# The first stage of a two-block transformer kernel: halves of 512 columns, a linear weight by weight, x scaled ahead of turning

## Chip, core and metric

One NeuronCore of a Trainium2 chip runs the whole program in one launch. The metric is the device time of one execution in microseconds (us). All arithmetic is float32; the large products are made of three products of float32 parts each (a high part in the engine's rounded format `fp32r`, and a low part that is the rest), so each weight and each activation has to be split into a high and a low part before TensorE may use it.

## The reference, cut to what matters

Two transformer blocks on `x` of 512 tokens by 1024 features, one batch. Only the beginning concerns this change:

```python
cond = silu(c)                                 # c: 1024 numbers
mod = cond @ w_ada[i] + b_ada[i]               # w_ada[i]: 1024 x 6144
sh1, sc1, gt1, sh2, sc2, gt2 = split(mod, 6)   # six vectors of 1024
h = rmsnorm(x, g_mix[i]) * (1 + sc1) + sh1     # modulate
cq = rmsnorm(h @ w_dq, g_q)                    # 1024 -> 384
q = cq @ w_uq                                  # 384 -> 8 heads x 192
ckv_kr = h @ w_dkv                             # 1024 -> 256 + 64
kv = rmsnorm(ckv_kr[..., :256], g_kv) @ w_ukv  # 256 -> 8 heads x 256
```

The angles of the rotary embedding (sine and cosine of position times frequency) are computed too. Behind this come attention, its output product, two feed-forward parts, a windowed attention, and the second block; the change leaves them alone.

## The kernel before, in words

The kernel holds x turned, with features on the partitions (`X`, 8 chunks of 128 features by 512 tokens). Each engine has its own program, written out by hand in order; an engine waits on named counts (`wait_ge`), in that order, so whatever stands behind a waiting instruction on its engine waits too. `Slots` hands out PSUM banks and small tiles in turn.

Weights are loaded by SyncE in the order of `PLAN` into three raw buffers (`SLOT`, `OLD`: a buffer is loaded again once its old content is used). ScalarE makes each weight's high part (`act_split`), VectorE the low part (`dve_split`), TensorE uses both.

The first stage, `*_begin` (lines 996 to 1087): x (2 MB) is loaded as one piece, turned by TensorE and copied out by ScalarE; ScalarE squares it, GpSimd sums the squares, TensorE sums them over partitions, and the reciprocal roots are spread over the partitions by a diagonal and a product (`R`). Of the two vectors that the first norm needs, the scale (vector 1) is made on VectorE in eight steps of 128x1024 (`dve_ada`), each a multiply and add with one column of silu(c), then summed over partitions by TensorE; the shift (vector 0) is made on TensorE as row products (`pe_row`). Each is loaded in four pieces of 1 MB. `dve_normed` then forms x times gain times `R` chunk by chunk, ScalarE adds the shift and makes the high part, VectorE the low part, for the first 256 tokens and then for the others.

The first linear, `dq`, is 1024 to 384: two weight units of four chunks. `pe_linear` goes by halves of the tokens on the outside and by weights inside: 4 x 36 products of 128x256. `dkv` follows in the same way, then `uq` (blocks of two heads; two of them here), then `ukv` in two blocks. TensorE's order is in `pe_mla_in` (line 1268), VectorE's in `dve_mla_in` (1353), GpSimd's in `pool_mla_in` (1405).

Three more vectors of `w_ada` (2, 4, 3) are made beside this: `BESIDE` has their 24 pieces of 128x1024. GpSimd's queue loads a piece (`pool_beside`, 719), VectorE takes it in one step (`dve_beside`, 730). The first eight pieces are vector (0, 2). TensorE sums it in `pe_columns(e, 0, 2)` (699), which waits for the eighth, and which stands in its order between the second `uq` block and `ukv`.

GpSimd computes the angles in `pool_begin` (1094), some 25 instructions of 128x512.

Of the kernel before, what the change touches and what calls it, by code (L numbers as in the profile page):

```python
# [146 lines left out]
def bass_two_blocks(nc, A, out):  # L147
    ctx = ExitStack()
    with ctx:
# [63 lines left out]
        XIN = sb([128, 4, D], F32, AR)  # L213
        V1 = sb([115, 128], F32, AR + 16 * KB)
# [150 lines left out]
        ada(0, 1)  # L365
        ada(0, 0, kind="p")
# [92 lines left out]
        FIRST, LAST = 8, WT[WX["mo"][3]]["p"]  # L459
        SLOT, OLD, held = [], [], {}  # L460
        for p in range(len(PLAN)):
            SLOT.append((p - FIRST - 1) % 2 if FIRST < p <= LAST else p % NRAW if p <= FIRST else (p - LAST) % NRAW)
            OLD.append(held.get(SLOT[p]))
            held[SLOT[p]] = p
        BESIDE = [(0, v, k) for v in (2, 4, 3) for k in range(8)]
# [55 lines left out]
        c_in, const_in, x_in, vec_in = count("c_in"), count("const_in"), count("x_in"), count("vec_in")  # L521
# [423 lines left out]
        def dve_add_x(e, T, j, hf, b, key, scale, before, mods=()):  # L945
# [9 lines left out]
                  mods=[(mod, (0, 1)), (mod, (0, 0))], h_free=lambda hf: (), h32=None)  # L955

        def act_vectors(e):
            A_ = {"c": A["c"].rearrange("b (j p) -> (b j) p", p=128),
# [13 lines left out]
            for name, (r, k) in rows.items():  # L972
                if name == "bq":
# [4 lines left out]
            e.dma_start(V2[:, :], A["b_ada"].rearrange("l (j p) -> (l j) p", p=128)).then_inc(vec_in, by=16)  # L978
            e.dma_start(VEC[:, 115:116], A["k_invf"]).then_inc(vec_in, by=16)
            e.dma_start(POS[:, :], A["positions"].to_broadcast([128, S])).then_inc(vec_in, "all", by=16)  # L980

        def pe_row(e, p, l, v, u):
            raw = raw_of(p, 2, D)
            e.wait_ge(landed[SLOT[p]], p)
            e.wait_ge(cond, "silu")
            for kk in range(2):
                k = 2 * u + kk
                for hf in range(2):
                    if k == 0:
                        banks.take(("row", hf), (copied, ("row", hf)), keep=True)  # L990
                        e.wait_for(banks.free(("row", hf)))
                    t = e.matmul(PS[0:1, banks["row", hf], :], SILUC[:, k:k + 1], raw[:, kk, 512 * hf:512 * hf + 512],
                                 start=k == 0, stop=k == 7)
            t.then_inc(acc, ("row", p))

        def pe_begin(e):
# [16 lines left out]
            pe_row(e, 4, 0, 0, 0)  # L1013
            pe_row(e, 5, 0, 0, 1)
            e.wait_ge(misc, "ones")
            pe_sums(e, "n0", 0, lasthf=F, add=ssq_pool)
            pe_sums(e, "n0", 1, lasthf=F, add=ssq_pool)
            pe_mod(e, 0, 1)
            pe_row(e, 6, 0, 0, 2)
            pe_row(e, 7, 0, 0, 3)  # L1020
            b = banks.take("row", (mod, (0, 0)))
            e.wait_for(banks.free("row"))
            for hf in range(2):
                e.wait_ge(copied, ("row", hf))
                for j in range(4):
                    t = e.matmul(PS[:, b, 4 * hf + j:4 * hf + j + 1],
                                 TMP[ta["row", hf]][0:1, 128 * j:128 * j + 128], ones[0:1, 0:1], start=True, stop=True)
                t.then_inc(acc, ("row", "t", hf))
                banks.open(("row", hf))
            for hf in range(2):  # L1030
                pe_R(e, n0, hf)
                banks.open(("R", "n0", hf))

        def act_begin(e):
            act_vectors(e)
            e.wait_ge(acc, "c")
            e.activation(SC[:, :], PS[:, banks["c"], 0:8], ACT.Exp, scale=-1.0).then_inc(misc_act, "exp")
            for j in range(8):
                e.wait_ge(acc, ("x", j))
                e.activation(X[:, j, :], PS[:, banks["x", j], :], ACT.Copy).then_inc(x_init, j)  # L1040
                e.wait_ge(x_init, j)
                act_square(e, "n0", j, F, X[:, j, :], add=ssq_pool)
            act_mod(e, 0, 1)
            act_root(e, "n0", 0, D)
            act_root(e, "n0", 1, D)
            act_split(e, 0)
            e.wait_ge(acc, ("row", 7))
            for hf in range(2):
                s = ta.take(("row", hf), (acc, ("row", "t", hf)))
                e.wait_for(ta.free(("row", hf)))  # L1050
                e.activation(TMP[s][0:1, :], PS[0:1, banks["row", hf], :], ACT.Copy).then_inc(copied, ("row", hf))
            act_normed(e, n0, 0, ALL)
            act_split(e, 1)
            act_normed(e, n0, 1, ALL)
            ta.hand([(h_lo, ("n0", 7, 1))], 4)
            ta.only(0, 1, 2, 4)

        def dve_begin(e):
# [4 lines left out]
            e.memset(ZERO, 0.0).then_inc(misc, "zero")  # L1063
            e.wait_ge(misc_act, "exp")
# [5 lines left out]
            for _ in range(4):  # L1070
                dve_item(e)
# [4 lines left out]
            e.wait_ge(misc, "columns")  # L1076
            dve_mod_lo(e, 0, 1)
            dve_diag(e, "n0", 0)
            dve_diag(e, "n0", 1)
            dve_mod(e, 0, 1)  # L1080
            dst = MOD[:, 0, 0:8]
            dve_split(e, 0)
            e.wait_ge(acc, ("row", "t", 1))
            e.tensor_tensor(dst, PS[:, banks["row"], 0:8], dst, ALU.add).then_inc(mod, (0, 0))
            dve_normed(e, n0, 0, ALL)
            dve_split(e, 1)
            dve_normed(e, n0, 1, ALL)
# [6 lines left out]
        def pool_begin(e):  # L1094
            for j in range(1, 7):
                add_square(e, "n0", j, F, add=ssq_pool)
# [8 lines left out]
            e.wait_ge(vec_in, "all")  # L1105
# [3 lines left out]
            for dst, quarter in ((SIN, 0.0), (COS, 0.25)):  # L1109
                ts(PA[:, :], PB[:, :], 1.0 / TWO_PI, quarter, ALU.mult, ALU.add)  # L1110
# [200 lines left out]
        def act_mla_in(e):  # L1311
            sums0 = lambda N: [(acc, ("sum", N, 0)), (acc, ("sum", N, 1))]
# [2347 lines left out]
```

## Time and profile before

| | |
|---|---|
| time, median of 3 runs | 2256.89 us (2255.12 to 2258.03) |
| the profiled execution | 2252.95 us |
| its span in the profile | 2250.9 us |
| mean granted TensorE clock | 0.992 |
| TensorE busy | 2181.1 us, 97% of the span |
| VectorE, ScalarE, GpSimd busy | 63%, 43%, 8% |
| moved by DMA | 245.70 MB, 109 GB/s in the mean |

The profile is of one execution. The page gives for each engine its busy time and for each group of instructions count and mean duration; the chain that ended last is followed back from the last instruction and says, for each moment, what the end was waiting for. A line of the kernel such as L66 is that of a helper, so all products have L66, all activations L72. "PE" is TensorE, "DVE" VectorE, "ACT" ScalarE, "POOL" GpSimd, "SP" SyncE.

### The profile page before, as it was taken

To read this page: it belongs to the slowest core of one execution; us is meant where nothing else is said; L and a number is where in the kernel's file an instruction comes from. 1 tells how busy PE (TensorE), PEld (TensorE's weight loads), DVE (VectorE), ACT (ScalarE), POOL (GpSimd) and SP (SyncE) were. 2 spreads that over 40 slices of the span, in tenths; PEclk is the share of its full clock that TensorE was granted. 3 is DMA by queue.
4 is the path that set the end of the run, shared out by engine and by line. 5 is a ranking of instruction groups with operands and counts; after the bars stand their busy time and mean duration, and the time that the engine had idled before them with its cause. 6 is when DMAs were issued, how large, how long until landed. Compare 5 with 4: busy or idle time off the path is not lost.

```text
span 2250.9 us, 31890 instructions
## 1 busy us (share of the span) xinstructions
PE 2181.1 (97%) x13239; PEld 1927.5 (86%) x13239; DVE 1418.2 (63%) x2129; ACT 965.0 (43%) x1460; POOL 184.9 (8%) x159
## 2 busy tenths in 40 slices
PE   6999999999999999999999999999999999999999
PEld 3877988888898898898898999997778889899998
DVE  5777565656577667565556667754665545666674
ACT  3556442213256645453443434434444334443443
POOL 7310000000032100000020000002012001000001
PEclk8999999999999999999999999999999999999999
DMA  6542245555521122332421332323112332233231
GB/s 237 162 145 90 89 169 187 187 189 185 187 83 57 39 66 85 113 99 90 132 75 62 113 105 96 109 89 111 52 47 80 122 105 64 66 122 106 88 108 56
DMA packets 128325, 245.70 MB, mean 109 GB/s; under 512 B 4843, under 2 KB 36934, under 8 KB 128054
## 3 DMA queue, kind: packets, MB, share of 16 engines
q1 hardware_dynamic: 123424, 228.02, 30.3%
q0 software_dynamic: 4096, 15.28, 2.1%
q8 instruction: 105, 1.72, 0.3%
q10 hardware_dynamic: 662, 0.37, 0.1%
q14 instruction: 38, 0.31, 0.0%
HBM read 241.56 MB, written 2.10 MB: 108 GB/s over the span
## 4 chain that ended last, share of the span: by engine, by line
PE 83%; DVE 9%; ACT 3%; DMA 2%; issue 2%; POOL 0%; SPq 0%; DVEq 0%; ACTq 0%
PE PS L66 82%; DVE t L75 5%; ACT t L72 3%; DVE t L83 2%; DVE t L86 1%; DMA t<-in_ffn_w_dram 1%; PE PS L69 1%; DMA t<-in_w_ada_dram 1%; DVE t L79 1%; DMA t<-in_w_ff_dram 0%; DVE t L92 0%; DVE t L80 0%; POOL t L75 0%; SPq L101 0%; DVE PS L75 0%
## 5 line engine op out<-in xcount | busy, mean ns | idle before, releaser
L66 PE MATMUL PS<-t,t 128*128 128x256 f32 (+4 forms) x12872 | 2134.1, 328 | 38.8 <-DMA t<-in_w_ada_dram 8.7
L66 PEld LDWEIGHTS PS<-t,t 128*128 128x128 f32 (+2 forms) x12872 | 1884.0, 188 | 285.0 <-issue 50.4
L72 ACT ACTIVATE t<-t 128x1024 fp32r<-128x1024 f32 (+7 forms) x738 | 654.3, 903 | 935.2 <-DVE t L75 462.1
L75 DVE TENSOR_TENSOR t<-t,t 128x1024 fp32r<-128x1024 f32 (+9 forms) x693 | 778.2, 1139 | 377.6 <-ACT t L72 330.6
L72 ACT ACTIVATE t<-PS 128x512 f32<-128x512 f32 (+4 forms) x327 | 174.9, 549 | 216.8 <-PE PS L66 166.1
L75 POOL TENSOR_TENSOR t<-t,t 128x512 f32<-128x512 f32 (+2 forms) x71 | 86.2, 1215 | 1091.2 <-ACT t L72 932.9
L75 DVE TENSOR_TENSOR t<-t,PS 128x512 f32<-128x512 f32 (+2 forms) x134 | 83.1, 625 | 145.5 <-PE PS L66 139.2
L72 ACT ACTIVATE t<-t,t 128x256 fp32r<-128x256 f32 (+5 forms) x220 | 115.8, 535 | 95.7 <-DVE t L83 44.8
L83 DVE SCALAR_TENSOR_TENSOR t<-t,t,t 128x1024 f32<-128x1024 f32 (+2 forms) x157 | 144.4, 926 | 16.7 <-DMA t<-in_w_ada_dram 11.0
L83 DVE SCALAR_TENSOR_TENSOR t<-PS,t,t 128x512 f32<-128x512 f32 (+3 forms) x128 | 82.1, 648 | 87.8 <-PE PS L66 82.2
L75 DVE TENSOR_TENSOR t<-t 128x512 f32<-128x512 f32 (+4 forms) x104 | 74.2, 714 | 16.2 <-ACT t L72 15.8
L83 DVE SCALAR_TENSOR_TENSOR t<-PS,t 128x512 f32<-128x512 f32 (+1 forms) x84 | 49.3, 610 | 53.1 <-PE PS L66 53.1
L69 PE MATMUL PS<-t,t 128*128 128x128 f32 (+1 forms) x367 | 56.9, 297 | 26.3 <-DVE t L79 8.3
L69 PEld LDWEIGHTS PS<-t,t 128*128 128x128 f32 (+1 forms) x367 | 45.5, 153 | 33.4 <-issue 11.3
L83 DVE SCALAR_TENSOR_TENSOR t<-t,t,PS 128x256 f32<-128x256 f32 (+1 forms) x117 | 54.4, 488 | 17.1 <-PE PS L66 14.1
L79 DVE TENSOR_SCALAR t<-t,t 128x128 f32<-128x128 f32 (+5 forms) x163 | 59.3, 394 | 4.5 <-DMA t<-in_w_ada_dram 2.5
L79 POOL TENSOR_SCALAR t<-t 128x512 f32<-128x512 f32 x28 | 46.5, 1662 | 74.3 <-DVE t L86 50.0
L79 POOL TENSOR_SCALAR t<-t,t 128x512 f32<-128x512 f32 x13 | 23.9, 1853 | 327.8 <-DVE t L83 312.8
L86 DVE CUSTOM_DVE_ANT_0 t<-PS,t 128x128 f32<-128x128 f32 (+1 forms) x112 | 38.4, 352 | 13.8 <-PE PS L66 13.7
L75 DVE TENSOR_TENSOR t<-PS,t 128x512 fp32r<-128x512 f32 (+2 forms) x40 | 24.9, 633 | 31.8 <-ACT t L72 24.7
L101 POOL DMA_DIRECT2D t<-in_k_dist_dram x1 | 0.5, 543 | 421.5 <-PE PS L66 421.5
L72 ACT ACTIVATE t<-PS,t 128x2 f32<-128x2 f32 (+3 forms) x48 | 21.5, 453 | 26.2 <-PE PS L66 22.0
(30 smaller groups left out, 166.9 us busy)
## 6 DMA issues: line engine op xcount, KB each, us to landing
t<-in_w_ff_dram SPq DMA_DIRECT2D x64, 1024.0 KB, 5.2
t<-in_ffn_w_dram SPq DMA_DIRECT2D x60, 1024.0 KB, 5.1
t<-in_w_ada_dram SPq DMA_DIRECT2D x36, 1024.0 KB, 6.4
t<-in_w_ada_dram POOLq DMA_DIRECT2D x24, 512.0 KB, 4.5
t<-in_w_in_dram SPq DMA_DIRECT2D x12, 1024.0 KB, 5.1
t<-in_swa_w_qkv_dram SPq DMA_DIRECT2D x6, 1024.0 KB, 5.7
t<-in_ffn_w_dram SPq DMA_DIRECT2D x8, 768.0 KB, 4.4
t<-in_w_in_dram SPq DMA_DIRECT2D x24, 256.0 KB, 3.6
```

The lines of the kernel that those rows point to most:

```text
L66: return Instr(self.real and self.real.matmul(o, lhs, rhs, start=start, stop=stop, **more))
L69: return Instr(self.real and self.real.transpose(o, src, ident))
L72: return Instr(self.real and self.real.activation(o, src, func, **more))
L75: return Instr(self.real and self.real.tensor_tensor(o, a, b, op))
L79: return Instr(self.real and self.real.tensor_scalar(o, a, s1, s2, op0))
L83: return Instr(self.real and self.real.scalar_tensor_tensor(o, a, s, b, op0, op1))
L86: return Instr(self.real and self.real.tensor_tensor_reduce(**more))
L101: return Instr(self.real and self.real.dma_start(o, src))
```

## The change

What it does, part by part:

- SyncE loads x in four pieces and the two vectors in four halves of 512 columns, (1,0), then (0,0) and (1,1), then (0,1) (vector, half), four pieces of 512 KB each, between the first weights, into tiles of their own, with no wait. The vectors leave `PLAN`.
- VectorE makes both vectors, `dve_first`: 32 steps of 128x512. The row products go.
- VectorE squares x as loaded and sums over features in one instruction for 128 tokens (`tensor_tensor_reduce`). ScalarE multiplies x, tokens on partitions, with its reciprocal root (`XSC`), TensorE turns this too, ScalarE applies the gain as it copies out (`act_gain`), for the upper four chunks in a second pass (`act_gain_again`). `R` and its diagonals go, for this norm.
- The first linear goes weight by weight (`pe_dq`): unit 0 for both token halves, then unit 1 for both. Products of the last vector halves stand in between. Four products whose result nothing uses (`warm`) stand ahead.
- GpSimd's angles start with the positions, which are loaded first on ScalarE's queue; two pieces of `BESIDE` are loaded between sine and cosine.
- The two single `dve_beside` steps in VectorE's `dq` and `dkv` parts go, and two come behind its second `uq` block.

```diff
-        ada(0, 1)
-        ada(0, 0, kind="p")
...
-        FIRST, LAST = 8, WT[WX["mo"][3]]["p"]
+        FIRST, LAST = 0, WT[WX["mo"][3]]["p"]
...
+        FIRST_PARTS = {0: ((1, 0),), 1: ((0, 0), (1, 1)), 2: ((0, 1),)}
...
+        def dve_first(e, v, ch, ks):
+            buf, tile = (ACC if v else ACC0)[:, 512 * ch:512 * ch + 512], FIRST_TILES[v, ch]
+            for k in ks:
...
+                    e.tensor_scalar(buf, tile[:, k, :], c, None, ALU.mult).then_inc(ada_acc, (0, v, ch, k))
+                else:
+                    e.wait_ge(ada_acc, (0, v, ch, k - 1))
+                    e.scalar_tensor_tensor(buf, tile[:, k, :], c, buf, ALU.mult, ALU.add).then_inc(ada_acc, (0, v, ch, k))
...
         def act_begin(e):
             act_vectors(e)
...
+            e.wait_ge(x_sq, 3)
+            e.activation(RS[:, 0:4], RS[:, 0:4], ACT.Sqrt, bias=EPSC, scale=1.0 / D).then_inc(root, "n0")
+            e.wait_ge(recip, "n0")
+            for t4 in range(4):
+                e.activation(XSC[:, t4, :], XIN[:, t4, :], ACT.Copy, scale=RS[:, t4:t4 + 1]).then_inc(x_gain, t4)
             for j in range(8):
                 e.wait_ge(acc, ("x", j))
                 e.activation(X[:, j, :], PS[:, banks["x", j], :], ACT.Copy).then_inc(x_init, j)
...
+            act_gain(e, LOWER)
             act_split(e, 0)
+            act_gain(e, (4, 5))
+            act_first_hi(e, 0, LOWER)
+            act_gain(e, (6, 7))
+            act_first_hi(e, 1, LOWER)
+            act_gain_again(e, UPPER)
             act_split(e, 1)
+            act_first_hi(e, 0, UPPER)
+            act_first_hi(e, 1, UPPER)
...
+            dve_first(e, 0, 0, range(2))
+            dve_first_columns(e, 1, 0)
+            dve_first(e, 0, 0, range(2, 6))
+            dve_at["vec"] = (0, 0)
             dve_split(e, 0)
+            dve_first(e, 0, 0, range(6, 8))
+            dve_first_columns(e, 0, 0)
+            dve_lowered(e, 0, LOWER)
+            dve_first(e, 1, 1, range(4))
+            dve_lowered(e, 1, LOWER)
+            dve_first(e, 1, 1, range(4, 8))
+            dve_first(e, 0, 1, range(2))
+            dve_first_columns(e, 1, 1)
+            dve_first(e, 0, 1, range(2, 4))
             dve_split(e, 1)
+            dve_first(e, 0, 1, range(4, 8))
+            dve_first_columns(e, 0, 1)
+            dve_lowered(e, 0, UPPER)
+            dve_lowered(e, 1, UPPER)
...
             for hf in range(2):
                 if hf:
                     dve_diag(e, "cq", 0, place=DIAG[0][0])
-                    dve_beside(e)
...
                     dve_diag(e, "cq", 1, place=DIAG[0][1])
-                    dve_beside(e)
...
             dve_uq(e, 1, WX["ukv"][0], after0=ck, after1=kr)
+            dve_beside(e, 2)
             dve_columns(e, 0, 2)
...
+            for t4 in range(4):
+                e.dma_start(XIN[:, t4, :], A["x"][0, 128 * t4:128 * t4 + 128, :]).then_inc(x_in[t4], "x", by=16)
```

## Rows read from the trace of the kernel before

**Rows 1.** The page: the span, and the chain that ended last by engine.
```profile
span 2250.9 us, 31890 instructions
...
PE 83%; DVE 9%; ACT 3%; DMA 2%; issue 2%; POOL 0%; SPq 0%; DVEq 0%; ACTq 0%
```

**Rows 2.** The chain of waits from 0 to 140: start us, us, what.
```profile
49.27 7.84 PE PS L66 x36
...
58.21 42.38 PE PS L66 x319
...
110.10 2.06 issue
...
114.15 22.11 PE PS L66 x90
```

**Rows 3.** Timeline of ScalarE from 71 us: start, us, instruction [idle before, releaser].
```profile
72.31 0.38 ACT L72 ACTIVATE t<-PS 128x256 f32<-128x256 f32 x1 [0.61 <-PE PS L66]
```

**Rows 4.** Windows: each engine's busy time, then PEclk, DMA share, GB/s.
```profile
5.00:10.00 5.00, 0.35 (x2) 0.35 (x3) 0.54 (x3) 1.46 (x2) 0.00 (x0) 1.00 1.03 407
10.00:15.00 5.00, 5.00 (x26) 5.00 (x25) 2.04 (x2) 4.07 (x8) 1.64 (x1) 1.00 1.04 363
```

**Rows 5.** Timeline of TensorE from 9 us: x is turned.
```profile
9.65 6.17 PE L69 MATMUL PS<-t,t 128*128 128x128 f32 x32 [5.60 <-DMA t<-in_x_dram]
```

**Rows 6.** Groups by shape on ScalarE and VectorE: count, busy us, mean ns, idle before.
```profile
L72 ACT ACTIVATE t<-t,t 128x1024 f32<-128x1024 f32 x4 | 4.6, 1149 | 2.2 <-DVE t L79 2.2
L72 ACT ACTIVATE t<-PS 128x512 f32<-128x512 f32 x220 | 128.9, 591 | 179.6 <-PE PS L66 133.9 <-PE PS L69 25.9 <-issue 8.6
L72 ACT ACTIVATE t<-PS,t 128x512 f32<-128x512 f32 x6 | 3.9, 686 | 8.6 <-PE PS L66 5.1 <-PE PS L69 3.2 <-DVE t L95 0.2
L72 ACT ACTIVATE t<-t,t 128x512 f32<-128x512 f32 x20 | 14.4, 720 | 17.4 <-DVE t L79 14.3 <-DVE t L95 2.9
L72 ACT ACTIVATE t<-t 128x1536 fp32r<-128x1536 f32 x18 | 26.5, 1475 | 13.3 <-PE PS L66 9.3 <-DMA t<-in_mla_w_dq_dram 4.0
L72 ACT ACT_TABLE_LOAD x15 | 19.2, 1283 | 8.1 <-issue 7.9
...
L75 DVE TENSOR_TENSOR t<-t,t 128x1024 fp32r<-128x1024 f32 x168 | 204.8, 1222 | 44.2 <-ACT t L72 38.7
L75 DVE TENSOR_TENSOR t<-t,t 128x1536 fp32r<-128x1536 f32 x18 | 31.7, 1768 | 31.1 <-ACT t L72 30.9
L79 DVE TENSOR_SCALAR t<-t,t 128x1024 f32<-128x1024 f32 x15 | 11.2, 750 | 2.7 <-DMA t<-in_w_ada_dram 2.5
L86 DVE CUSTOM_DVE_ANT_0 t<-PS,t,t 128x512 f32<-128x512 f32 x8 | 6.0, 751 | 0.3
L83 DVE SCALAR_TENSOR_TENSOR t<-t,t,t 128x512 f32<-128x512 f32 x8 | 5.4, 744 | 0.0
```

**Rows 7.** Timelines of GpSimd and of VectorE at three places.
```profile
17.13 2.12 POOL L75 TENSOR_TENSOR t<-t,t 128x512 f32<-128x512 f32 x1
...
50.47 0.48 DVE L83 SCALAR_TENSOR_TENSOR t<-t,t,t 128x256 fp32r<-128x256 f32 x1
...
77.12 1.28 DVE L83 SCALAR_TENSOR_TENSOR t<-t,t,t 128x1024 f32<-128x1024 f32 x1
```

**Rows 8.** Line L83 on VectorE from 16 to 29: ns min/median/max, first and last start.
```profile
L83 DVE SCALAR_TENSOR_TENSOR t<-t,t,t x6: 1511/2099/2167, 16.2 to 27.0; 128x1024 f32<-128x1024 f32 x6
```

**Rows 9.** Windows of 1 us, columns as in rows 4.
```profile
49.00:50.00 1.00, 0.73 (x3) 0.71 (x3) 0.96 (x3) 0.33 (x1) 1.00 (x1) 0.50 0.00 0
...
114.00:115.00 1.00, 0.89 (x3) 0.76 (x3) 1.00 (x3) 0.28 (x1) 0.00 (x0) 0.50 0.72 240
...
117.00:118.00 1.00, 1.00 (x6) 0.83 (x5) 1.00 (x3) 1.00 (x3) 0.00 (x0) 0.94 0.00 0
```

**Rows 10.** Timeline of VectorE from 98 to 118.
```profile
109.96 2.27 DVE L75 TENSOR_TENSOR t<-t,t 128x2048 fp32r<-128x2048 f32 x1
...
115.39 1.41 DVE L75 TENSOR_TENSOR t<-t,t 64x512 fp32r<-64x512 f32 x2
```

More of the change, by code:

```diff
@@ L213, in bass_two_blocks @@
         XIN = sb([128, 4, D], F32, AR)
+        JUNK = [sb([128, D], F32, o_lo + 4 * i * KB) for i in range(2)]
+        XSC = sb([128, 4, D], F32, o_hi + 8 * KB)
+        HN0 = sb([128, 8, S], F32, o_h + 16 * KB)
+        ACC0 = sb([128, D], F32, o_tmp)
         V1 = sb([115, 128], F32, AR + 16 * KB)
@@ L977, in act_vectors @@
                     e.dma_start(V1[r:r + k, :], A_[name]).then_inc(vec_in, by=16)
[L978 to L994, printed above, removed]
+            e.dma_start(V2[:, :], A["b_ada"].rearrange("l (j p) -> (l j) p", p=128)).then_inc(vec_in, "all", by=16)
@@ new lines, in pe_first_columns @@
+        def pe_first_columns(e, v, ch):
+            b = banks.take(("mod", 0, v, ch), (mod, (0, v, "sum", ch)))
+            e.wait_for(banks.free(("mod", 0, v, ch)))
+            e.wait_ge(ada_acc, (0, v, ch, 7))
+            e.wait_ge(misc, "ones")
+            for j in range(4):
+                t = e.matmul(PS[:, b, j:j + 1], (ACC if v else ACC0)[:, 512 * ch + 128 * j:512 * ch + 128 * j + 128],
+                             ones[:, 0:1], start=True, stop=True)
+            t.then_inc(acc, ("mod", 0, v, ch))
@@ L1023, in pe_begin @@
[L1023 to L1032, printed above, removed]
+            pe_x_scaled(e, LOWER)
@@ new lines, in pe_begin, with pe_x_scaled @@
+            pe_first_columns(e, 1, 0)
+            pe_x_scaled(e, UPPER)
+            b = banks.take("warm", (acc, "warm"))
+            e.wait_for(banks.free("warm"))
+            e.wait_ge(landed_first[0, 0][1], (0, 0))
+            for _ in range(4):
+                t = e.matmul(PS[:, b, :], ones, X[:, 0, :], start=True, stop=True)
+            t.then_inc(acc, "warm")
+            pe_first_columns(e, 0, 0)
+        def pe_x_scaled(e, chunks):
+            for j in chunks:
+                b = banks.take(("xs", j), (x_turned, j))
+                e.wait_for(banks.free(("xs", j)))
+                for t4 in range(4):
+                    e.wait_ge(x_gain, t4)
+                    t = e.transpose(PS[:, b, t4 * 128:(t4 + 1) * 128], XSC[:, t4, j * 128:(j + 1) * 128], ident)
+                t.then_inc(acc, ("xs", j))
@@ L1034, in act_begin, with act_first_hi @@
+        def act_first_hi(e, hf, chunks):
+            for j in chunks:
+                cs = COLS[hf]
+                if j in UPPER:
+                    e.wait_ge(x_gain, ("again", j))
+                e.wait_ge(x_turned, j)
+                e.wait_ge(mod, (0, 0, "sum", j // 4))
+                e.activation(HHI[:, j, cs], HN0[:, j, cs], ACT.Identity, bias=MOD[:, 0, j:j + 1]).then_inc(
+                    h_hi, ("n0", j, hf))
         def act_begin(e):
             act_vectors(e)
-            e.wait_ge(acc, "c")
@@ L1069, in dve_begin @@
             e.tensor_tensor(SILUC[:, :], PS[:, banks["c"], 0:8], SC[:, :], ALU.mult).then_inc(cond, "silu")
-            for _ in range(4):
-                dve_item(e)
+            dve_x_squares(e, range(2, 4))
+            dve_first(e, 1, 0, range(2))
+            e.wait_ge(root, "n0")
+            e.reciprocal(RS[:, 0:4], RS[:, 0:4]).then_inc(recip, "n0")
+            dve_first(e, 1, 0, range(2, 8))
             e.wait_ge(acc, "columns")
```

169 lines of the change are left out of this document (113 added, 56 removed).

## The prediction

> **What bounds the kernel now.** I read the page first: TensorE holds 83% of the chain that ended last [rows 1], so a change pays only where TensorE waits. Next the chain of waits in order of time, from 0 to 140 us. The reader is to see that TensorE does not work steadily before 49.27 (until then the chain is loads of `w_ada`, the row products and their copies), that the first unit of `dq` takes 7.84 us for 36 products, that from 58.21 it runs without a break to 100.6, and that a second hole comes at 110.10, 2.06 us before the `ukv` products [rows 2]. Then ScalarE's timeline: the last third of `dq` is copied out at 72.31, 0.61 us after waiting for TensorE, so `dq` ends at T = 72.3 [rows 3]. From T to the end of the first `ukv` block the rest of the program keeps its order, with one exception that the diff makes (below). So the change has two terms: A, how far T moves; B, what the exception costs.
>
> **Loads.** The queue now has x (2.1 MB), two vectors in four halves (2.1 MB each) and the weights between them, and no wait ahead of any. The queue moves 407 and 363 GB/s when it has enough to do [rows 4]; at 0.39 MB per us behind x (landed 9.65, when its turning starts [rows 5]) the halves have landed at about 15, 22.4, 27.8 and 35.2, `dq` at 17 and 29.8. Each of the steps below comes later than its data after 15 us, so loads stop setting the pace. That the smaller pieces cost nothing is bounded by the two rows: at the slower rate throughout the last half lands at 36.8, still unneeded.
>
> **A, step by step** (durations [rows 6] unless said).
> 1. Squares of x, four reductions of 1024 columns on VectorE. The trace has none of that width: bounds 1.22 (a subtraction of 1024) and 1.50 (twice the 512 one, 0.75); I take 1.37, between them. The last one ends at 11.4.
> 2. Table load 1.28, root and reciprocal 0.43: 13.2.
> 3. ScalarE scales x in four of 1.15: 17.8, copies the turned x out in eight of 0.59: 22.5. These eight stand in front of the gain, since the order is fixed. A bank for the first small products comes free only near their end; gain there at 23.2 (0.7, my estimate from four weight loads and two small adds).
> 4. Four gains from PSUM at 0.69: 26.0; the first weights' high part 1.48: 27.5; VectorE's low part 1.77: 29.3; two steps of the second half vector, 0.74 each: 30.8; its products and addition 1.0: 31.8; shift and low part of one chunk 1.0: TensorE starts `dq` at 32.8, where it was 49.27.
> 5. But the unit after it waits for the upper halves, and these go on VectorE after the lower ones. From 32.3: four low parts 2.0, eight steps of half (1,1) and two of (0,1) with four more low parts between them: 2.64 + 1.95 + 2.98 + 1.16 = 8.7, product and gain 0.5: 43.5. (A half vector costs one 0.38, half of the 0.75 of 1024, rounded up to 0.42 for its start, and seven 0.74: 5.6. Four cost 22.4. Before, VectorE had one vector, 0.75 + 7 x 1.28 = 9.7 us, and TensorE the other, so this adds 12.7 us of work to VectorE.)
> 6. ScalarE's gains again 4 x 0.72 = 2.9, weights 1.48, low part 1.77, four steps 3.0, product and addition 1.0, shift and low part 1.0: 11.2, and 54.7.
> 7. VectorE beside GpSimd. A step of 1024 takes 1.28 alone, and a median of 2.10 while GpSimd adds in SBUF (its addition 2.12) [rows 7, 8]: each such addition costs VectorE 0.8. Beside a GpSimd instruction with one tensor in, the 256-column steps keep their 0.48 [rows 7]. The table of angles used to start behind GpSimd's additions of squares; now it starts near 6 and its cosine half (three additions, 11 instructions, about 18 us) runs from about 31 to 49, just over steps 5 and 6. Bounds: 0 (all in VectorE's idle time) and 3 x 0.8 plus as much again for the one-input ones, 4.8. I take 2.2: 56.9.
> 8. TensorE has been idle for over 9 us then. Its granted clock is 0.50 when it starts at 49 (the 1.2 GHz level); after the hole at 110 it is 0.50 at 114 and up at 117 [rows 9]. The unit's first half took 7.84 before (bound above); 36 at the full pace of 0.12 would be 4.3 (below; 108 products from 58.21 to T). No product here is held by VectorE after the fourth, so about 3 us of low clock: 6.4. The second half at full pace 4.6. T' = 67.9.
> A = 67.9 - 72.3 = -4.4. Bounds from the open prices: -4.4 - 2.2 - 2.1 - 1 = about -10, and -4.4 + 2.6 + 1.4 = about 0. Removed row products, diagonals and the 16 normalising steps with R lay ahead of T and are replaced by the above, not added to it.
>
> **B, the exception.** Two steps of vector (0,2) used to stand in the `dq` and `dkv` stages, one at 77.12 with GpSimd idle (1.28), both off the chain. Now the sixth and seventh (counting from 0) stand behind VectorE's whole second `uq` block. TensorE asks for that vector with `pe_columns(0, 2)`, in order, ahead of `ukv`. Before, it was ready and TensorE waited only for the low part of `ukv` (109.96 + 2.27) [rows 10] and then 0.6 more for a bank. VectorE works without a pause from that part at 109.96 (and before it) to 116.8, where its last rotated part ends [rows 10]. Behind it come 2 x 1.28 and two pauses of 0.04: 119.5. Then eight small products, between 0.8 us (full clock) and 2.0 (low): the first `ukv` product at 120.3 to 121.5, I take 121.0, where it was 112.3 [rows 2]. Given back: the 0.6 wait at 113.5, and part of the low clock (0.50 from 114 to 117 [rows 9] cost 1.6; after the longer hole about 1.1 remains of it, as the small products start the recovery). B = 8.7 - 0.6 - 0.8 = +7.3, bounds 6 and 9. What is queued behind the waiting instruction: all of `ukv`, so ScalarE's and VectorE's copies too. It is not given back later in the block: from 114.15 TensorE ran 22.11 us with 90 products and no wait [rows 2]. SyncE's queue is not in it (both `ukv` weights are loaded), and GpSimd's two transfers for it go out with its rotations, whose result VectorE needs before them, so they have landed by then.
>
> **Sum.** -4.4 + 7.3 = +2.9 us. Against the profiled execution (2252.95, its span 2250.9) that is 2255.9; the median of the three runs, 2256.89, lies 3.9 above that execution, so I forecast 2259.8 for a median. A measurement of this kernel can tell about 0.2%, 4.5 us, from no change.
>
> **A rule of the Trainium skill beside rows 7 and 8.** The rows show both engines slowed, but not by the whole of the other's instruction: 2.10 where 1.28 + 1.27 would be 2.55. *SBUF — State Buffer*, on the shared port pair, says that a VectorE instruction with two SBUF inputs and a GpSimd one that reads SBUF exclude each other for a whole instruction. By that rule all two-input steps from 31 to 49 us would stretch, beside any reading GpSimd instruction, and the time would be about that of rival 1. In its full form the 0.48 row speaks against it [rows 7].
>
> **Rivals.**
> 1. Slower: GpSimd beside every two-input step. If each VectorE step on the path in 5 and 6 (about 12.5 us of them) took 2.10/1.28 = 1.64 times its length, step 7 costs 8.0 and not 2.2: T' = 73.7, A = +1.4, sum +8.7: 2265.6. It decides from a ratio of 1.3 on. For: the 2.10 median. Against: the 0.48 row.
> 2. Faster: B is not there, because VectorE gets through `uq` early enough or TensorE's wait is hidden in later slack. Then -4.4: 2252.5. Against: VectorE has no pause from 110 to 117 and TensorE none behind 114.
> 3. Faster: the stage follows the loads, ScalarE and VectorE never being late. Last half at 35.2, plus 1.5, 1.0, 1.0 and 11.0 for TensorE: T' = 49.7, A = -22.6, sum -15.3: 2241.6. Against: ScalarE's fixed row of 15 us after the root, and steps 5 and 6.
> 4. Faster: the mechanism holds with a shorter middle, A near -10 (its lower bound) and B at 6: 2252.9.
>
> **How the numbers follow.** Forecast 0.55, rival 1 0.18, rival 2 0.10, rival 3 0.07, rival 4 0.10. The forecast's own range is 2256 to 2264. Eight in ten: from 2250 to 2267, leaving out rival 3 and the far end of rival 1. Slower by over 0.2% (above 2261.4): rival 1 and a third of the forecast, 0.36. Faster (below 2252.4): rival 3, half of 2 and 4, and a little for what I mis-sized, 0.20. Within: 0.44.
>
> **What would show it.** Right: TensorE's first 256-column product near 33, a hole of 7 to 11 us before the second unit, the last `dq` copy on ScalarE at 66 to 69; then, between the last `uq` product and the first `ukv` one, 10 us of TensorE idle that ends with a 1024-column step, where 1.7 stood, and the span after it moved as a whole. Wrong: `dq` over by 60 (steps 5 to 7), or a `ukv` hole under 5 us (B). VectorE steps of 512 near 1.2 us would be rival 1; TensorE waiting for a load in the second unit, rival 3.

## The result and the profile after

The changed kernel takes 2269.91 us (median of 6 runs, 2267.88 to 2274.98) against 2257.46 for the kernel before on the same chip (6 runs): ratio 1.0053, 95% interval 1.0034 to 1.0071. It is slower by about 12.0 us; 2.9 us slower was the forecast, and the time lies outside the range.

The page after, where [rows 1] have 2250.9 us and TensorE at 83% of the chain:

```profile
span 2267.4 us, 31907 instructions
...
PE 81%; DVE 10%; ACT 4%; issue 2%; DMA 2%; POOL 0%; DVEq 0%; SPq 0%; ACTq 0%
```

The chain of waits from 0 to 160 us (start us, us, what). The reader is to see TensorE's pieces at 49.55, 60.78 and 125.06: each time the chain comes to it from VectorE's adding steps (L83), where [rows 2] had TensorE at work from 58.21 to 100.6.

```profile
14.26 1.28 ACT L72
16.09 4.75 ACT t L72 x5
...
34.00 1.04 PE PS L66 x8
...
46.83 1.58 DVE t L83
48.43 0.99 DVE t L83
49.55 1.85 PE PS L66 x8
51.81 3.94 ACT t L72 x5
...
60.78 1.85 PE PS L66 x8
...
64.38 40.51 PE PS L66 x283
...
122.25 1.29 DVE t L83
123.64 1.29 DVE t L83
125.06 35.08 PE PS L66 x160
```

ScalarE's timeline: the last copy of `dq`, which gives T, stood at 72.31 [rows 3] and now stands 4.3 us later.

```profile
76.62 0.38 ACT L72 ACTIVATE t<-PS 128x256 f32<-128x256 f32 x1 [0.61 <-PE PS L66]
```

TensorE's timeline (in brackets the idle time before and what ended it): `dq` starts at 36.48, its second unit at 64.38, and a hole of 11.83 us stands before the small products that sum vector (0,2) ahead of `ukv`.

```profile
36.48 8.32 PE L66 MATMUL PS<-t,t 128*128 128x256 f32 x45 [1.46 <-DVE t L83]
...
60.78 1.84 PE L66 MATMUL PS<-t,t 128*128 128x1 f32 x8 [4.19 <-DVE t L83]
64.38 48.85 PE L66 MATMUL PS<-t,t 128*128 128x256 f32 x318 [1.77 <-DVE t L83]
125.06 3.12 PE L66 MATMUL PS<-t,t 128*128 128x1 f32 x14 [11.83 <-DVE t L83]
```

In the kernel before, that hole was 1.74 us, and `ukv` started at 112.33:

```profile
112.33 13.03 PE L66 MATMUL PS<-t,t 128*128 128x512 f32 x48 [1.74 <-issue]
```

VectorE's timeline. The first row is the middle of step 5: eleven steps, seven of 512 columns and four of 256 (a row names the first form of its group), in 11.00 us.

```profile
38.41 11.00 DVE L83 SCALAR_TENSOR_TENSOR t<-t,t,t 128x512 f32<-128x512 f32 x11
...
112.03 2.76 DVE L75 TENSOR_TENSOR t<-t,t 128x512 fp32r<-128x512 f32 x2
...
122.25 2.67 DVE L83 SCALAR_TENSOR_TENSOR t<-t,t,t 128x1024 f32<-128x1024 f32 x2
128.65 0.16 DVE L75 TENSOR_TENSOR t<-t,PS 128x8 f32<-128x8 f32 x1 [3.73 <-PE PS L66]
```

GpSimd's timeline meanwhile, the cosine half of the angles; L79 and L80 have one tensor as input, L75 two.

```profile
34.82 4.90 POOL L79 TENSOR_SCALAR t<-t 128x512 f32<-128x512 f32 x3
39.80 1.57 POOL L75 TENSOR_TENSOR t<-t,t 128x512 f32<-128x512 f32 x1
41.45 1.81 POOL L79 TENSOR_SCALAR t<-t 128x512 f32<-128x512 f32 x1
43.35 1.29 POOL L75 TENSOR_TENSOR t<-t,t 128x512 f32<-128x512 f32 x1
44.73 1.54 POOL L79 TENSOR_SCALAR t<-t 128x512 f32<-128x512 f32 x1
46.35 1.49 POOL L75 TENSOR_TENSOR t<-t,t 128x512 f32<-128x512 f32 x1
```

A caution on the profiles: the execution profiled before (span 2250.9) was a quick one. TensorE's long product run starts at M = 213.05 before and at 227.56 after, and from there to the end it is 2037.9 before, 2039.8 after and 2040.2 in the first experiment, whose code there is the same. So 16.5 us between the spans overstate the difference; T and M are compared below, and times by the ratios.

### The profile page after: what moved, and what is told of

It is laid out like the page before. It is cut to its first block, busy times and chain, and to the rows that moved or that the text cites. A ratio compares the mean times of both kernels' runs of the same rounds, so it can differ in the third digit from the quotient of the medians.

```text
span 2267.4 us, 31907 instructions
## 1 busy us (share of the span) xinstructions
PE 2181.0 (96%) x13239; PEld 1939.1 (86%) x13239; DVE 1427.3 (63%) x2137; ACT 967.6 (43%) x1463; POOL 171.9 (8%) x153
## 4 chain that ended last, share of the span: by engine, by line
PE 81%; DVE 10%; ACT 4%; issue 2%; DMA 2%; POOL 0%; DVEq 0%; SPq 0%; ACTq 0%
PE PS L66 80%; DVE t L75 5%; ACT t L72 4%; DVE t L83 3%; DVE t L86 2%; DMA t<-in_ffn_w_dram 1%; PE PS L69 1%; DVE t L79 1%; DMA t<-in_x_dram 0%; DMA t<-in_w_ff_dram 0%; DVE t L92 0%; DVE t L80 0%; POOL t L75 0%; DVE t L95 0%; POOL t L79 0%
## 5 line engine op out<-in xcount | busy, mean ns | idle before, releaser
L66 PE MATMUL PS<-t,t 128*128 128x256 f32 (+3 forms) x12840 | 2129.0, 329 | 50.4 <-DVE t L83 25.6
L66 PEld LDWEIGHTS PS<-t,t 128*128 128x128 f32 (+1 forms) x12840 | 1891.2, 190 | 284.4 <-issue 60.3
L72 ACT ACTIVATE t<-t 128x1024 fp32r<-128x1024 f32 (+9 forms) x729 | 648.4, 906 | 925.1 <-DVE t L75 464.8
L75 DVE TENSOR_TENSOR t<-t,t 128x512 fp32r<-128x512 f32 (+9 forms) x690 | 778.1, 1144 | 384.4 <-ACT t L72 336.6
L72 ACT ACTIVATE t<-PS 128x512 f32<-128x512 f32 (+3 forms) x329 | 175.6, 550 | 226.1 <-PE PS L66 178.3
L75 DVE TENSOR_TENSOR t<-t,PS 128x512 f32<-128x512 f32 (+3 forms) x138 | 83.9, 612 | 154.1 <-PE PS L66 147.9
L72 ACT ACTIVATE t<-t,t 128x256 fp32r<-128x256 f32 (+6 forms) x228 | 121.4, 548 | 107.5 <-DVE t L83 45.7
L83 DVE SCALAR_TENSOR_TENSOR t<-t,t,t 128x256 fp32r<-128x256 f32 (+2 forms) x178 | 155.8, 889 | 11.8 <-ACT t L72 4.9
L75 POOL TENSOR_TENSOR t<-t,t 128x512 f32<-128x512 f32 (+2 forms) x65 | 72.6, 1117 | 1083.8 <-ACT t L72 921.3
L83 DVE SCALAR_TENSOR_TENSOR t<-PS,t,t 128x512 f32<-128x512 f32 (+3 forms) x128 | 82.2, 649 | 87.7 <-PE PS L66 82.1
L69 PE MATMUL PS<-t,t 128*128 128x128 f32 (+1 forms) x399 | 62.4, 300 | 31.1 <-ACT t L72 11.4
L75 DVE TENSOR_TENSOR t<-t 128x512 f32<-128x512 f32 (+4 forms) x104 | 74.2, 715 | 16.2 <-ACT t L72 15.8
L69 PEld LDWEIGHTS PS<-t,t 128*128 128x128 f32 (+1 forms) x399 | 50.1, 154 | 38.7 <-ACT t L72 14.6
L83 DVE SCALAR_TENSOR_TENSOR t<-PS,t 128x512 f32<-128x512 f32 (+1 forms) x84 | 49.3, 611 | 53.3 <-PE PS L66 53.3
L79 DVE TENSOR_SCALAR t<-t,t 128x128 f32<-128x128 f32 (+6 forms) x162 | 60.1, 400 | 2.0
L83 DVE SCALAR_TENSOR_TENSOR t<-t,t,PS 128x256 f32<-128x256 f32 (+1 forms) x101 | 46.9, 490 | 17.6 <-PE PS L66 15.0
L79 POOL TENSOR_SCALAR t<-t 128x512 f32<-128x512 f32 x28 | 48.6, 1735 | 74.2 <-DVE t L86 49.9
L79 POOL TENSOR_SCALAR t<-t,t 128x512 f32<-128x512 f32 x13 | 23.1, 1787 | 327.8 <-DVE t L83 312.8
L75 DVE TENSOR_TENSOR t<-PS,t 128x512 fp32r<-128x512 f32 (+2 forms) x39 | 25.1, 647 | 32.6 <-ACT t L72 28.4
```

The lines of the kernel that those rows point to most:

```text
L66: return Instr(self.real and self.real.matmul(o, lhs, rhs, start=start, stop=stop, **more))
L69: return Instr(self.real and self.real.transpose(o, src, ident))
L72: return Instr(self.real and self.real.activation(o, src, func, **more))
L75: return Instr(self.real and self.real.tensor_tensor(o, a, b, op))
L79: return Instr(self.real and self.real.tensor_scalar(o, a, s1, s2, op0))
L83: return Instr(self.real and self.real.scalar_tensor_tensor(o, a, s, b, op0, op1))
```

## The experiments

Two marks serve throughout: T (last `dq` copy on ScalarE) and M (start of the long product run on TensorE). A mark is read from one profiled execution. Ratios are against the kernel before, measured with them.

**1. The pair of side steps alone, from both sides.** In `e1` the changed kernel gets the order of side steps back:

```diff
                     dve_diag(e, "cq", 0, place=DIAG[0][0])
+                    dve_beside(e)
...
                     dve_diag(e, "cq", 1, place=DIAG[0][1])
+                    dve_beside(e)
...
-            dve_beside(e, 2)
             dve_columns(e, 0, 2)
...
-            pool_beside(e, 4)
+            pool_beside(e, 6)
...
-            pool_beside(e, 2)
             pool_rotate(e, ("qr", 1), F, COS)
```

> The changed kernel with the order of the side steps put back: one step of vector (0,2) in the dq part, one in the dkv part, none behind the second uq block, and GpSimd loads six pieces ahead of its rotations. Theory (two causes: the pair behind uq costs 10.3 us, the first stage itself 4.3): last dq copy stays near 76.6, the hole before ukv shrinks from 12 us to about 2, time 10 us below the changed kernel, so about 2 to 5 us above the one before. Rival (all of the loss is the first stage, the hole is only where a delay shows): the hole stays above 8 us, time within 3 us of the changed kernel.

`e2` is the kernel before with the reverse of this edit and nothing else.

> The kernel before with this part of the change alone: both side steps moved behind the second uq block, GpSimd's loads of them between its rotations. Theory: dq ends at 72.3 as before, TensorE waits about 12 us before ukv, time +10 us (+8 to +11). Rival (the move costs only in company of the new first stage, whose VectorE is late): under +4 us.

Measured: `e1` 2257.22 us, ratio 1.0002 (0.9993 to 1.0012); `e2` 2270.0, ratio 1.0057 (1.0042 to 1.0072). TensorE's timelines, `e1` first, then `e2`:

```profile
115.80 26.69 PE L66 MATMUL PS<-t,t 128*128 128x512 f32 x116 [1.74 <-issue]
```

```profile
122.67 27.39 PE L66 MATMUL PS<-t,t 128*128 128x1 f32 x112 [11.85 <-DVE t L83]
```

The hole comes and goes with this edit. Between the medians' ratios B is 1.0053 - 1.0002, or 11.5 us, on the new first stage, and 12.9 on the old one. The rest of the change, term A, is +0.5 us (-1.6 to +2.7): no measurable difference.

**2. GpSimd's angles.** `e4` holds the cosine half back until the first stage's last half vector is there; `e3` leaves the angles out altogether (both tables filled with a constant, so the rotations are not those of the reference).

```diff
                 if dst is COS:
                     pool_beside(e, 2)
+                    e.wait_ge(mod, (0, 0, "sum", 1))
```

```diff
-            for dst, quarter in ((SIN, 0.0), (COS, 0.25)):
...
+            for dst in (SIN, COS):
...
+                e.memset(dst[:, :], 0.5).then_inc(angle, step[0], "all")
```

> The changed kernel with the cosine half of GpSimd's angles held until the last part of the shift vector is added, so that it runs beside the dq products and not beside VectorE's steps. Theory (GpSimd's two- and one-input instructions stretch VectorE's steps): VectorE's stretch from the first low part to the last step of half (1,1) falls from 13.5 us to about 10, last dq copy from 76.6 to about 73.5, time -3 us. Rival (the steps are as long for another reason, loads or instruction gaps): no change in that stretch, time within 1 us, or later if the sine table is now late for the rotations.

> The changed kernel without the two angle tables (GpSimd fills them with a constant instead of 22 instructions; the rotations use the constant). It bounds what GpSimd's work costs beside both halves of the stage. Theory: VectorE's stretch from the first low part to the last step of half (1,1) takes about 10.2 us as with the cosine held, and the part ahead of it is 1 to 2 us shorter too (the sine half runs there): first dq product near 35, last dq copy 69 to 71. Rival (only the cosine half matters): first dq product at 36.4 as before.

Measured: `e4` 2264.41 us, ratio 1.0034 (1.0021 to 1.0047), T = 70.72. `e3`, a single execution: 2261.68, T = 68.64. VectorE's and ScalarE's timelines of `e3`, where the reader is to compare the same eleven steps and T:

```profile
10.89 1.22 DVE L86 CUSTOM_DVE_ANT_0 t<-t 128x1024 f32<-128x1024 f32 x1
...
36.16 7.07 DVE L83 SCALAR_TENSOR_TENSOR t<-t,t,t 128x512 f32<-128x512 f32 x11
```

```profile
68.64 0.38 ACT L72 ACTIVATE t<-PS 128x256 f32<-128x256 f32 x1 [0.61 <-PE PS L66]
```

7.07 us where the changed kernel takes 11.00 for the same seven and four steps: a ratio of 1.56. One by one, the three steps that begin while a two-input instruction of GpSimd runs (40.27, 43.38, 46.83) are longer by 0.90, 1.07 and 0.81 us, four that begin beside a one-input one by 0.22 to 0.35, and four keep their length. The first of the three, 0.75 us when alone:

```profile
40.27 1.65 DVE L83 SCALAR_TENSOR_TENSOR t<-t,t,t 128x512 f32<-128x512 f32 x1
```

In all, the table costs 76.62 - 68.64 = 8.0 us of T. TensorE's timeline of `e3` against the one above shows where:

```profile
34.68 8.42 PE L66 MATMUL PS<-t,t 128*128 128x256 f32 x48 [1.46 <-DVE t L83]
43.38 3.99 PE L66 MATMUL PS<-t,t 128*128 128x1 f32 x32 [0.28 <-DVE t L83]
...
57.41 47.85 PE L66 MATMUL PS<-t,t 128*128 128x256 f32 x318 [1.77 <-DVE t L83]
```

- 1.8 us ahead of `dq` (34.68 for 36.48), where the sine half runs. Other executions with the same order up to there start `dq` between 35.41 and 36.70, so this part is 0.7 to 2.0.
- 4.4 us in VectorE's steps beside the cosine half: the eleven (3.9) and the five ahead of them (0.5).
- 0.8 us in the four small products and their additions. TensorE comes to them after 3.90 us of waiting, and they take 1.85 us at the low clock; in `e3` it waited 0.28 us.
- 1.0 us in the second unit: from its start to T 12.24 us, 11.23 in `e3`, where the clock was back at 1.00 from 60.7, 3.3 us after the start and not 5.6.

Held back, the cosine half leaves the eleven steps alone (7.08 in `e4`) and 2.1 of the 8.0 remain, for what GpSimd does before it. Of the 5.9 us that T is earlier, 4.0 are left at M (223.60) and 4.3 in the ratios, whose intervals overlap. The cosine half now runs beside `dkv`'s first low parts and opens a wait of 1.07 on TensorE:

```profile
71.75 36.88 PE L66 MATMUL PS<-t,t 128*128 128x256 f32 x238 [1.07 <-DVE t L79]
```

**3. TensorE's clock in `dq`'s hole.** `e5` puts 8 and 7 products of 128x512, whose result nothing uses, ahead of the small products of the last two half vectors.

```diff
                         if (u, hf, n) == (0, 1, 0):
+                            pe_warm(e, "first", 8, (h_lo, ("n0", 3, 1)))
                             pe_first_columns(e, 1, 1)
...
                 if u:
+                    pe_warm(e, "dq", 7, (ada_acc, (0, 0, 1, 0)))
                     pe_first_columns(e, 0, 1)
```

> The changed kernel with 8 and 7 more 128x512 products whose result nothing uses, in TensorE's two idle stretches of the first linear (before the second part of the gain, and before the second part of the shift). Theory (part of the loss is the low clock after a hole): both groups of four small products take about 1.0 us and not 1.85, and the second unit has at most 2 us at clock 0.50 where it had 6; last dq copy 3 to 4.5 us earlier, time -3 to -4.5. Rival (TensorE is not late there, VectorE is): below 1 us.

Measured: 2267.7 us, ratio 1.005 (1.0033 to 1.0066), T = 75.75, only 0.9 earlier, and in this execution `dq` had started 1.1 earlier (35.41). The small products ahead of the second unit did get faster:

```profile
61.62 1.02 PE L66 MATMUL PS<-t,t 128*128 128x1 f32 x8 [0.41 <-DVE t L83]
```

1.02 where 1.84 stood. But the clock was 0.50 again in part of the second unit: 0.72 from 64 to 66 and 0.50 from 66 to 68. And the first group overran: I had sized a product at 0.43 us where one takes 0.87 (experiment 5), and VectorE waited 2.76 us for the sum behind it, 0.84 in the changed kernel. My expectation missed, and the run doesn't price the clock.

**4. Moving the request instead of the steps.** `e6` and `e13` leave the pair where the change puts it and move TensorE's request for vector (0, 2) behind the first and behind the fourth head of `ukv`; `e14` is `e13` with `e4`'s wait.

```diff
-            pe_columns(e, 0, 2)
             for hb, w in enumerate(WX["ukv"]):
...
                     t.then_inc(acc, ("kn", h))
+                    if h == 3:
+                        pe_columns(e, 0, 2)
```

> The changed kernel with TensorE's eight small products of vector (0,2) one place later: behind the first key head of ukv instead of ahead of ukv. Nothing else moves; the pair stays late on VectorE. Theory (what costs is that ukv stands in TensorE's order behind a vector that VectorE ends late): the hole before ukv shrinks from 12 us to about 2, TensorE then waits behind the first head for VectorE instead, since the first head takes only about 1.3 us of the 12; so no more than 1 to 2 us are won, time -1 to -2 us against the changed kernel. Rival (the place of the vector, whichever, is worth the whole 10 us): -8 or more.

> As the run with the small products behind the first key head (which won nothing), but behind the fourth: TensorE has about 6 us of ukv products of its own before it asks for vector (0,2), and the banks suffice without VectorE's copies of them. Theory (the cost is TensorE's order, and the first head was too little to cover the wait): the hole before ukv is 2 us as before the change, the one at the small products under 3 us, time -7 to -10 against the changed kernel. Rival (VectorE itself is what ukv waits for, so that a late pair costs wherever it is asked for): within 3 us of it.

> The small products behind the fourth key head, and the cosine half held until the shift is done; the side pair stays where the change put it. Theory: the two mends add, 2270 - 9 - 5.5 = 2255 to 2257, level with the kernel before and not below it. Rival (taking the pair out of the dkv part frees VectorE there, so this beats the run with the pair put back): 2252 or less.

Measured: `e6` 2271.56 us, 1.0061 (1.0046 to 1.0075); `e13` 2265.53, 1.0040 (1.0027 to 1.0053); `e14` 2259.11, 1.0010 (1.0000 to 1.0020). TensorE in `e6`, then in `e13`:

```profile
117.45 2.90 PE L66 MATMUL PS<-t,t 128*128 128x512 f32 x6 [4.53 <-DVE t L75]
124.67 35.56 PE L66 MATMUL PS<-t,t 128*128 128x1 f32 x162 [4.31 <-DVE t L83]
```

```profile
117.47 30.52 PE L66 MATMUL PS<-t,t 128*128 128x512 f32 x132 [4.53 <-DVE t L75]
```

`e6` splits one hole into two and wins nothing. `e13` loses the wait for the pair, yet keeps a hole of 4.53 ended by `ukv`'s low part: it ends at T + 41.1 instead of T + 40.0. So GpSimd's rotation, late behind the two loads, costs there as well (next section). M - T is 146.2 in `e13`, 141.3 in `e1`, 150.9 in the changed kernel: half of B is won back. VectorE now waits 2.10 us for the small products behind the fourth head. `e13`'s gain over the changed kernel was smaller than expected and its interval overlaps that one's. `e14` came out about level with the kernel before, as expected, 2 us above the upper end of what I had written down.

**5. TensorE's clock in the hole before `ukv`.** `e11` and `e15` put 26 and 12 unused products into it (the edit of `e15`):

```diff
             pe_uq(e, 1, after0=kr)
+            pe_warm(e, "uq", 12)
```

> The changed kernel with 26 more 128x512 products whose result nothing uses, behind the second uq block, so that TensorE is busy for about 11 of its 12 idle us. VectorE's late pair stays. Theory (of the 10 to 13 us, about 3 to 4 are low clock behind the hole, not the wait): the eight small products take 1.8 us or less and not 3.6, no stretch at clock 0.50 behind 125, time -3 to -4 against the changed kernel. Rival (the whole is the wait, the small products are as long at any clock): within 1 us.

> The changed kernel with 12 unused 128x512 products of 0.87 us behind the second uq block, which end near 123.7, before VectorE's late pair (125). Theory (of the 10 to 13 us about 3 to 4 are low clock behind the hole): the eight small products take about 1.8 us and not 3.6, clock 1.00 from 125 on, time -3 to -4 against the changed kernel, 2266. Rival (the whole is the wait): within 1 us.

`e11`: 2276.19 us, 1.0082 (1.0069 to 1.0095). It overran: I had sized a product at 0.43 us, and one took about 0.87 at full clock, so TensorE was still busy with them at 130 (window of 2 us; TensorE's busy time and records first, PEclk third from the end):

```profile
130.00:132.00 2.00, 2.00 (x6) 0.95 (x5) 0.00 (x0) 0.00 (x0) 0.00 (x0) 1.00 0.00 0
```

`e15`: 2268.08 us, 1.0043 (1.0030 to 1.0057). The small products came at 123.85 at full clock, and the clock fell all the same behind them:

```profile
125.00:126.00 1.00, 1.00 (x10) 0.95 (x10) 0.17 (x2) 0.00 (x0) 0.00 (x0) 1.00 0.97 303
...
127.00:128.00 1.00, 1.00 (x4) 0.72 (x4) 1.00 (x1) 0.23 (x1) 0.00 (x0) 0.50 0.52 209
```

M - T is 149.7, 1.2 less than in the changed kernel; by the ratios it is 2.3 us quicker, with overlapping intervals. So of B only 1 to 2 us is low clock that products in the hole avoid; most of it is the wait.

**6. Both causes removed, and on from there.** `e9` is `e1` and `e4` together. `e10` adds vector 0 as row products on TensorE (VectorE does 16 steps instead of 32, the four `warm` products go, and the small products of (1,1) and ScalarE's gains move a little); `e12` and `e16` add to `e9` unused products as in `e5`, 3 and 12, and 1 and 5.

```diff
-            dve_first(e, 0, 0, range(2))
+            pe_first_row(e, 0)
+            pe_row_columns(e, 0)
...
+            act_row(e, 0)
```

> The changed kernel with both mends: the side steps back in the dq and dkv parts, the cosine half of the angles held until the shift is done. Theory (the two costs are separate and add): e1 was 12.7 us and e4 5.5 us below the changed kernel; together 17 to 18 below it, 2252 us, 4 to 5 us under the kernel before; last dq copy near 70.7. Rival (the second mend is eaten when the first is in, since the angles then run beside dkv and the side steps): no better than e1, 2257.

> As the run with both mends, and the shift vector made by TensorE as row products of 1x512, as before the change, from the new half tiles: VectorE has 16 steps of 512 and not 32. Theory (the rest of the first stage is bound by VectorE's own work on two vectors): the second unit of dq starts 6 us or more sooner than in the run with both mends, last dq copy at 62 to 66, time 2244 to 2248. Rival (ScalarE's fixed order bounds it, so that VectorE's work can go without gain): within 2 us of the run with both mends.

> The run with both mends, and 3 and 12 unused 128x512 products in TensorE's two idle stretches of the first linear. Theory (low clock at the second unit and at the small products ahead of it costs 2 to 3 us, as the 2.2 us of the run with unused products alone said): last dq copy from 71.2 to about 69, time 2252 to 2253. Rival: the dkv split, late beside GpSimd's angles, takes it back: 2255 as without.

> The run with both mends (side pair back, cosine held) and 1 and 5 unused 128x512 products of 0.87 us in TensorE's two idle stretches of the first linear; the second group ends before the last half of the shift. Theory (low clock at the second unit costs 2 to 3 us): four small products take 1.0 and not 1.84, second unit at clock 1.00, last dq copy near 69 where it was 71.2, time 2252 to 2253 against 2254.9. Rival (the dkv low part, late beside GpSimd's angles, takes it back): 2255, with a gap of TensorE behind dq of 2 us or more.

| | median us | ratio, 95% | T | M |
|---|---|---|---|---|
| `e9` | 2254.86 | 0.9988 (0.9979 to 0.9997) | 71.19 | 211.12 |
| `e10` | 2254.6 | 0.9991 (0.9981 to 1.0001) | 70.58 | 212.31 |
| `e12` | 2256.55 | 0.9997 (0.9989 to 1.0006) | 76.15 | 216.63 |
| `e16` | 2250.16 | 0.9968 (0.9956 to 0.9981) | 71.05 | 211.53 |

`e10`: half of VectorE's steps gone, and T only 0.6 earlier. ScalarE now waits for the row, and VectorE for ScalarE (both timelines, ScalarE first):

```profile
52.04 0.59 ACT L72 ACTIVATE t<-PS 1x512 f32<-1x512 f32 x1 [4.01 <-PE PS L66]
```

```profile
54.04 1.76 DVE L75 TENSOR_TENSOR t<-t,t 128x1536 fp32r<-128x1536 f32 x1 [8.60 <-ACT t L72]
```

`e12` overran like `e11` (T + 5). `e16`, the quickest, beats the kernel before by 0.32% and `e9` too in the medians. Its unused products are not shown to be the reason: the small ones take 1.02 rather than 1.84, yet T and M are `e9`'s, and the clock is 0.50 from 60 to 62 all the same. In the profiles its lead lies behind M (2036.9 us to the end, 2039.4 in `e9`), where both have the same code. Its gain over `e9` stays unexplained; their intervals overlap.

## Why the prediction was wrong

B happened as described and was priced too low; A's gain did not come. Together they put the sum off by 9.1 us: A came out +0.5 instead of -4.4, B +11.5 instead of +7.3 (by the ratios of `e1` and of the change).

**The step of A that failed is step 7**, "VectorE beside GpSimd", taken at 2.2 us with 4.8 as its upper bound. `e3` shows 8.0. What step 7 counted, VectorE's steps beside the cosine half, took 4.4, inside its bounds: 2.8 beside the three two-input instructions (2.4 in its sum) and the rest beside the others. For these I had let one row stand, the 0.48 of a 256-column step [rows 7]; a step of 512, 0.75 when alone, is stretched beside them, as at 44.84, where an L79 runs on GpSimd from 44.73 to 46.27:

```profile
44.84 1.09 DVE L83 SCALAR_TENSOR_TENSOR t<-t,t,t 128x512 f32<-128x512 f32 x1
```

Two parts stood at nothing in it: the sine half ahead of `dq` (1.8), and the low clock that TensorE meets after the longer waits (1.8, in experiment 2's last two parts).

With 8.0 in its place the forecast's A would have been +1.4, inside the measured interval. That is rival 1's number, but it came out by luck. Rival 1 had every step of 5 and 6 stretched by 1.64 and nothing else; four of the eleven keep their length, and so do the four of step 6, which run when GpSimd has ended the table (51.9) and are as long as in `e3`:

```profile
57.45 3.18 DVE L83 SCALAR_TENSOR_TENSOR t<-t,t,t 128x512 f32<-128x512 f32 x4
```

The *SBUF — State Buffer* page of the Trainium skill, "Who interferes with whom", says that a VectorE instruction with two SBUF inputs contends with a GpSimd one that reads SBUF, and calls the port pair that they share an exclusive lock. On which instructions meet, the trace agrees with it and not with me. On the price it agrees nearly for GpSimd's two-input instructions: the steps at 40.27 and 46.83 end 0.55 us after it does (41.37, 47.84), where alone they take 0.75, and 2.10 stands in [rows 8] for a full 2.55. Beside one-input instructions of 1.5 to 2.3 us a step grew by 0.35 at most, far from the whole instruction.

By the marks, forecast and measured (the cumulative delay in brackets):

| step | forecast | after |
|---|---|---|
| 1: last square over (ScalarE goes on) | 11.4 | 14.26 (+2.9) |
| 2, 3: scaling starts, x copied out | 13.2, 22.5 | 16.09, 24.25 (+1.8) |
| 4: TensorE starts `dq` | 32.8 | 36.48 (+3.7) |
| 5: upper gain ready | 43.5 | 51.8 (+8.3) |
| 6, 7: second unit starts | 56.9 | 64.38 (+7.5) |
| 8: T | 67.9 | 76.62 (+8.7) |

Of the 8.7 us, 5.8 are step 7 (8.0 - 2.2). The other 2.9 stand in `e3` too, whose T of 68.64 compares with 65.7 without step 7.

- Step 1: a square of 1024 takes 1.23 in `e3` and up to 1.62 beside GpSimd, so the width was priced rightly (1.37 between) and the start missed: the first piece of x landed at 7.73, 1.8 us later than the sum needs (11.4 less four squares), and the silu steps that stand between the squares (about 0.9 us, one of them 0.56 where it is 0.17 in `e3`) were left out.
- Step 5 has the largest slip, 4.6 us: 3.9 are the eleven steps above and 1.3 the small products (1.85 us where 0.5 stood; 1.0 at full clock), less 0.6 elsewhere.
- Steps 6 and 7 took 12.6 us where 11.2 and 2.2 stood. I had put GpSimd's whole price there; it fell on steps 1 to 5 and on the clock. The 1.4 above 11.2 are in `e3` as well: small products and their additions took 2.6 us where 1.0 stood.
- Step 8: 12.2 us where 11.0 stood. The granted clock was 0.50 (1.2 GHz) from 64 to 70 and not for about 3 us, after TensorE's idle time ahead of 64.38:

```profile
68.00:70.00 2.00, 2.00 (x11) 2.00 (x11) 0.00 (x0) 0.27 (x2) 0.00 (x0) 0.51 0.00 0
70.00:71.00 1.00, 1.00 (x11) 1.00 (x10) 0.18 (x1) 0.69 (x2) 0.00 (x0) 1.00 0.00 0
```

Part of A's miss is the yardstick: with the old first stage, `e2` has T = 74.22 where [rows 3] have 72.31. From 74.22 the changed kernel's A is +2.4 in the profile; the medians say +0.5.

**Of B the price was low.** What the prediction said happens: VectorE gets to the pair without a pause, TensorE waits for its sum with `ukv` behind it (rival 2 is out). In marks behind T: the pair ends at T + 48.3 (forecast T + 47.2), the eight small products at T + 52.0 (forecast T + 48.7), where `ukv` used to start at T + 40.0. Two terms were mis-sized:
- The small products took 3.6 us (125.06 to 128.65). I bounded them by 0.8 and 2.0, from no row; at the low clock four alone take 1.85.
- A pair of low parts at 112.03 took 2.76 us, 1.64 in my sum. The change issues two loads ahead of GpSimd's last rotation, a product with two inputs, and so pushes the rotation beside the pair:

```profile
111.21 1.12 POOL L101 DMA_DIRECT2D t<-in_w_ada_dram  x2
112.34 1.29 POOL L75 TENSOR_TENSOR t<-t,t 128x512 f32<-128x512 f32 x1
```

Before, the rotation was over at 108.22 and the two issues themselves stood beside the same pair, which took 1.64; its second half (108.69) ran wholly beside them in 0.68 us, as long as the second half in the changed kernel with GpSimd idle:

```profile
107.73 1.64 DVE L75 TENSOR_TENSOR t<-t,t 128x512 fp32r<-128x512 f32 x2
108.16 1.12 POOL L101 DMA_DIRECT2D t<-in_w_ada_dram  x2
```

`e1` has the old order and 1.65, `e2` the new one and 2.77. So it is the rotation and not the issuing; I took the transfers to be landed in time, and so they were, but what their new place moves beside VectorE I didn't price. The small products end 12.0 us behind the old start of `ukv`, and M - T is longer by 9.6 than in `e1`, so some 2.4 are given back (1.4 in my sum). The medians' 11.5 is 1.9 more, and on the old first stage M - T grows by 13.2 (153.9 in `e2`, 140.7 before); these remainders are about the width of the intervals and stay open.

Loads were not the limit behind the first piece of x (rival 3 is out): from 9.06 us to 160 no wait of the chain ends with a load, and the queue moved 414 GB/s from 8 to 10. Rival 4, both terms at their quick ends, failed with both terms. Rival 1 had A's size by luck, as said; with B at 7.3 its total of 2265.6 lay 4.3 below the time.

## What to carry to other kernels

A side engine's program is part of the price of a reorder: before steps with two SBUF inputs go onto the path, lay GpSimd's timeline beside them, over the whole stage and not only where they are thickest. Here a step that began while a two-input instruction of GpSimd ran cost 0.8 to 1.1 us more, beside a one-input one up to 0.35 more, and the longer waits of TensorE that followed cost 1.8 us of low clock on top. A sum that another engine asks for in order must be finished before that engine gets there; two 1.3 us steps moved behind a block cost 11.5 us, since the small products at the low clock and a rotation displaced by their loads come on top of the steps themselves and of what stands ahead of them. When an old order hides such a step off the chain, leave it there, and price a term from the state in which it will run (clock, neighbours), not from its row in quiet surroundings.

## What the runs showed of the hardware

- A run of eleven two-input VectorE steps takes 7.07 us with GpSimd idle (`e3`) and 11.00 in the changed kernel: 2.8 of the difference is beside three two-input instructions of GpSimd, 1.1 beside one-input ones.
- A two-input VectorE instruction of 512 columns that ran wholly beside two DMA issues on GpSimd kept its 0.68 us (before). The pair it belongs to takes 1.64 there and 2.76 with a two-input product of GpSimd in its midst (changed kernel).
- An unused float32 product of 128x512 takes about 0.87 us at full clock, twice what I had sized from the kernel's products.
- Eight small-product records (four products of one column) take 1.02 us at full clock and 1.84 to 1.85 at the 1.2 GHz level.
- In `e15` the clock was 1.00 through the filled stretch and 0.50 from 126.6 to 130.0, though TensorE had had no hole longer than 1.45 us since 63.4. In `e16` it was 0.50 in the second unit behind 5 unused products, with holes of 2.1 and 2.0 us ahead. In `e11`, whose unused products ran right up to the small ones, it stayed at 1.00 behind them (136.2 to 144). What decides this was not settled.
